# Hybrid decoder step on one core: x split ahead of the queries, q as three fp32r products, the norm broadcast ahead of u's 64-row tile, four gate jobs ahead of the state space products

## The reference

```
xn = rmsnorm(x, lp['norm1_g'])
u, q, k, v, qm, gates = jnp.split(xn @ lp['w_in'], split_at, axis=-1)
y_ssm, h_re, h_im = s5_scan(u, h0_re, h0_im, lp)
z = jax.nn.gelu(y_ssm)
z = z * jax.nn.sigmoid(z @ lp['w_glu'] + lp['b_glu'])
...
o_swa = sink_band_attention(q, kk, vv, True, lp['sinks'], rel_table)
o_mem = mem_attention(qm.reshape(...), mem_k, mem_v)
g = jax.nn.sigmoid(gates.reshape(b, t, N_BRANCHES, D_MODEL))
merged = (g[:, :, 0] * (z @ lp['w_br_ssm'])
          + g[:, :, 1] * (o_swa @ lp['w_br_swa'])
          + g[:, :, 2] * (o_mem @ lp['w_br_mem']))
x = x + merged @ lp['w_out']
x = x + hier_moe(rmsnorm(x, lp['norm2_g']), lp)
```

## Time and profile before

| | us |
|---|---|
| median of 3 runs (823.11 to 824.79) | 823.43 |
| profiled execution, its own time | 825.33 |
| its span, first to last instruction | 823.5 |
| TensorE busy | 764.2 (93%) |
| VectorE busy | 375.8 (46%) |
| ScalarE busy | 237.8 (29%) |
| GpSimd busy | 75.1 (9%) |

### The profile page before, as it was taken

One profiled execution on the slowest core, in us unless ns is written; L12 is line 12 of the kernel. 1 busy time (PEld: TensorE's weight loads), 2 busy tenths in 40 slices (PEclk: granted clock), 3 DMA queues, 4 the chain that ended last, 5 costly groups with the idle time before them and its releaser, 6 DMA issues. The chain is left out here.

```text
span 823.5 us, 11842 instructions
## 1 busy us (share of the span) xinstructions
PE 764.2 (93%) x4899; PEld 576.5 (70%) x4899; DVE 375.8 (46%) x677; ACT 237.8 (29%) x404; POOL 75.1 (9%) x105
## 2 busy tenths in 40 slices
PE   8999999999999999989999999998999978787864
PEld 6887899999998766779999988884333323222321
DVE  2589689903723666366244276454112111111117
ACT  1413531303563535262343232120111101100113
POOL 0100220001003020100000000011011110001000
PEclk9999999999999999999999999999999999999997
DMA  8652254314336452400241582089999999999957
GB/s 344 223 179 93 77 86 127 110 65 156 101 123 239 174 236 96 154 1 1 103 167 52 196 349 99 26 326 416 422 427 422 423 426 425 424 424 425 424 177 301
DMA packets 34554, 186.15 MB, mean 226 GB/s; under 512 B 5979, under 2 KB 6251, under 8 KB 17512
## 3 DMA queue, kind: packets, MB, share of 16 engines
q1 hardware_dynamic: 22288, 148.22, 44.9%
q0 software_dynamic: 11344, 35.24, 12.8%
q10 hardware_dynamic: 864, 1.88, 0.6%
HBM read 176.17 MB, written 17.22 MB: 235 GB/s over the span
## 5 line engine op out<-in xcount | busy, mean ns | idle before, releaser
L540 PE MATMUL ps<-sb 128*64 128x512 f32 (+16 forms) x2334 | 423.5, 436 | 47.9 <-DMA sb<-in_wexp 28.4
L540 PEld LDWEIGHTS ps<-sb 128*64 128x64 f32 (+6 forms) x2334 | 246.8, 160 | 198.9 <-issue 152.6
L540 PE MATMUL ps<-sr 128*128 128x288 f32 (+2 forms) x2160 | 302.6, 300 | 0.1
L540 PEld LDWEIGHTS ps<-sr 128*128 128x128 f32 x2160 | 289.8, 188 | 7.2 <-issue 1.4
L551 PEld LDWEIGHTS ps<-sb 128*128 128x128 f32 (+3 forms) x405 | 41.8, 140 | 31.9 <-issue 28.3
L2232 DVE SCALAR_TENSOR_TENSOR sb<-sb,ps 128x256 f32<-128x256 f32 x16 | 6.7, 421 | 124.9 <-ACT sb L1511 124.9
L551 PE MATMUL ps<-sb 128*128 128x128 f32 (+3 forms) x405 | 52.7, 269 | 3.1 <-issue 1.5
L1981 DVE TENSOR_TENSOR sr<-sb,sr 128x2048 fp32r<-128x2048 f32 (+2 forms) x23 | 39.9, 1754 | 28.4 <-ACT sr L1265 14.6
L2241 DVE COPY sb<-ps 128x1024 f32<-128x1024 f32 (+1 forms) x16 | 19.1, 1191 | 67.4 <-PE ps L540 67.4
L1969 DVE SCALAR_TENSOR_TENSOR sb<-sb,ps 128x576 f32<-128x576 f32 x24 | 18.1, 752 | 58.6 <-PE ps L540 58.6
L1173 ACT ACTIVATE sb<-ps 128x576 f32<-128x576 f32 (+4 forms) x29 | 22.9, 789 | 70.9 <-PE ps L540 48.9
(11 more groups left out here) (261 smaller groups left out, 465.1 us busy)
## 6 DMA issues: line engine op xcount, KB each, us to landing
sb<-in_wexp SPq DMA_DIRECT2D x96, 1024.0 KB, 27.5
sb<-in_wstream SPq DMA_DIRECT2D x33, 1024.0 KB, 4.9
sb<-in_mkT POOLq DMA_DIRECT2D x8, 512.0 KB, 9.9
sb<-in_mv POOLq DMA_DIRECT2D x8, 512.0 KB, 7.0
sb<-expert_rows SPq DMA_DIRECT2D x8, 512.0 KB, 7.5
sb<-in_x SPq DMA_DIRECT2D x4, 512.0 KB, 14.1
sb<-k_pad POOLq DMA_DIRECT2D x8, 256.0 KB, 6.1
sb<-in_x POOLq DMA_DIRECT2D x4, 512.0 KB, 9.6
```

The costliest lines, as they stand in the source:

```text
L540: return signed(nc.tensor.matmul(*a, **kw))
```

## The change

1. x is split in nine pieces instead of three, and earlier: the high parts on ScalarE behind u4's copy, the low parts on VectorE inside the input matrices, right behind the normed x.
2. Blocks 3 and 4 get high and low parts as well, and q0 to q3 become split jobs of 48 fp32r matmuls. q0 no longer waits slab by slab, but for all low parts of x and of block 3. kT stands between q0 and q1 as before.
3. rsb stands ahead of u4 on TensorE.
4. g00 and g01 stand ahead of K0, and g02 and g03 between K1 and VT0. g04 to g07 stay behind B3.
5. The low parts on VectorE: blocks 3 and 4 ahead of and between the tables of Y, 5 between those of VT, 6 and 7 behind the repacking of u, 8 behind B's copies, 9 behind the seventh `inside`, 10 behind the advances, 11 and 12 behind the scan. The high parts on ScalarE move alike; its wait for `scanned` stays behind g07.

```diff
-X_PARTS = [(O_XH, 0, 6 * T + TH), (O_SM, 6 * T + TH, TH), (O_SM + TH, 7 * T, T)]
-EARLY_HI = {5: O_Z + 256, 6: O_A + 8704, 7: O_A + 10752, 8: O_Z + 256, 9: O_A + 8704, 10: O_A + 10752, 11: O_O, 12: O_Z + 256}
+X_PARTS = [(O_XH + kt * T, kt * T, T) for kt in range(6)]
+X_PARTS += [(O_XH + 6 * T, 6 * T, TH), (O_SM, 6 * T + TH, TH), (O_SM + TH, 7 * T, T)]
+XS = [f"x{part}" for part in range(len(X_PARTS))]
+EARLY_HI = {3: O_UG, 4: O_A, 5: O_A + 2048, 6: O_UG, 7: O_A + 10752, 8: O_Z + 256, 9: O_A + 8704, 10: O_A + 10752, 11: O_O, 12: O_Z + 256}
...
-LOWS = [5, "x1", "x2", "x0"] + [what for what in HIGHS[4:] if not (isinstance(what, tuple) and what[0] == "w")] + [("w", b) for b in range(4)]
+LOWS = [what for what in HIGHS if not (isinstance(what, tuple) and what[0] == "w")] + [("w", b) for b in range(4)]
...
-    jobs = [f"u{t}" for t in range(TT)] + ["rsb"] + [f"kv{t}" for t in range(TT)]
-    jobs += ["q0", "kT"] + [f"q{m}" for m in range(1, 4)] + [f"K{i}" for i in range(2)]
+    jobs = [f"u{t}" for t in range(TT - 1)] + ["rsb", "u4"] + [f"kv{t}" for t in range(TT)]
+    jobs += ["q0", "kT"] + [f"q{m}" for m in range(1, 4)] + ["g00", "g01"] + [f"K{i}" for i in range(2)] + ["g02", "g03"]
-    jobs += [f"g0{d}" for d in range(8)] + [f"qm{m}" for m in range(4)] + [f"Y{i}" for i in range(4)]
+    jobs += [f"g0{d}" for d in range(4, 8)] + [f"qm{m}" for m in range(4)] + [f"Y{i}" for i in range(4)]
...
-            take("u4")
-            side_by_side("u4", O_XG, [(wu[0], 256), (wu[1], 256)]).then_inc(ps_ready, 1)
-            owed.append((w_used, 2))
...
+            take("u4")
+            side_by_side("u4", O_XG, [(wu[0], 256), (wu[1], 256)]).then_inc(ps_ready, 1)
+            owed.append((w_used, 2))
...
-            for m in range(4):
-                if m % 2 == 0:
-                    w = weights()
-                columns(f"q{m}", w + (m % 2) * 128, 256, O_X, KT).then_inc(ps_ready, 1)
-                if m == 0:
...
+            def turn_keys():
+                pe.wait_ge(kv_sb, TT)
+                take("kT")
+                for t in range(TT):
+                    last = turn_tile(pat(pair("kT"), t * 128, (1, ROWS[t])),
+                                     at(O_KV + t * 256, (1, 128), pn=ROWS[t]), at(O_ID, (1, ROWS[t]), pn=ROWS[t]))
+                last.then_inc(ps_ready, 1)
+
+            pe.wait_ge(lo_ready, LOWS.index(XS[-1]) + 1)
+            split_block(["q0", "q1"], turn_keys)
+            split_block(["q2", "q3"])
+            split_block(["g00", "g01"])
...
+            split_block(["g02", "g03"])
...
-            for d in range(0, 8, 2):
+            for d in range(4, 8, 2):
...
+            for part in range(7):
+                act.wait_ge(xn_ready, part + 1)
+                high_x(part)
...
+                if t == 0:
+                    act.wait_ge(lo_ready, 1)
+                    act.wait_ge(xn_ready, KT)
+                    high_x(7)
+                    high_x(8)
+                    early_high(3)
+                if t == 1:
+                    early_high(4)
...
-                    act.wait_ge(xn_ready, KT)
-                    high_x(0)
-                if m == 2:
-                    act.wait_ge(ssm_built, 2)
-                    high_x(1)
-                    high_x(2)
                     early_high(5)
+            early_high(6)
+            gate_zero(0)
+            gate_zero(1)
+            act.wait_ge(up_sb, 4)
+            early_high(7)
+            filled(act, "K1")
+            gate_zero(2)
+            gate_zero(3)
             for i in range(4):
                 copy_out(f"VT{i}", at(A_VT + i * 1024, (1, 1024)), pat(pair(f"VT{i}"), 0, (1, 1024)), vt_sb)
             for i in range(4):
                 copy_out(f"U{i}", at(O_UG + i * 8 * NC, (4 * NC, 2), (1, 4 * NC)),
                          pat(pair(f"U{i}"), 0, (512, 2), (1, 4 * NC)), ug_sb)
 
-            act.wait_ge(up_sb, 4)
-            early_high(6)
-            early_high(7)
-            for d in range(8):
-                filled(act, f"g0{d}")
-                c.free(fn(at(O_TH + d * T, (TH, 2), (1, TH)), pat(pair(f"g0{d}"), 0, (512, 2), (1, TH)), ACT.Tanh, scale=0.5),
-                       f"g0{d}")
+            early_high(8)
+            early_high(9)
+            for d in range(4, 8):
+                gate_zero(d)
+                if d == 5:
+                    early_high(10)
                 if d == 7:
                     act.wait_ge(scanned, 1)
-                if d % 2:
-                    early_high(8 + d // 2)
+                    early_high(11)
...
+            for part in range(len(X_PARTS)):
+                low_x(part)
...
+            early_low(3)
             for hf in range(2):
+                if hf:
+                    early_low(4)
...
             for hf in range(2):
+                if hf:
+                    early_low(5)
...
-            early_low(5)
-
-            filled(dve, "q3")
-            low_x(1)
-            low_x(2)
+            early_low(6)
...
-            low_x(0)
...
-            early_low(6)
+            early_low(8)
...
             for j in range(1, 8):
                 inside(j)
-                if j == 4:
-                    early_low(7)
-            early_low(8)
+            early_low(9)
             for k in range(1, 8):
                 advance((8 * k - 1) * G, (8 * k + 7) * G, c64)
-            early_low(9)
+            early_low(10)
...
-            for b in (10, 11, 12):
+            for b in (11, 12):
```

More of the change, by code:

```diff
@@ L558, in columns @@
                     for kt in range(kts):
-                        if job == "q0" and half == 0:
-                            pe.wait_ge(xn_ready, kt + 1)
                         last = mm(pat(p, half * 512, (1, TH)), at(w + kt * wstep, (1, 128)),
@@ L572, in split_columns, with split_block @@
                 return last
-            def split_block(jobs):
+            def split_block(jobs, between=None):
                 b = blocks_taken[0]
@@ L580, in split_block @@
                     split_columns(job, EARLY_HI[b] + i * 128, w + i * 128).then_inc(ps_ready, 1)
+                    if i == 0 and between:
+                        between()
                 owed.append((w_used, 1))
@@ L639, in _ @@
             pe.wait_ge(ld["const"], 16)
-            for m in range(4):
-                if m % 2 == 0:
-                    w = weights()
-                columns(f"q{m}", w + (m % 2) * 128, 256, O_X, KT).then_inc(ps_ready, 1)
-                if m == 0:
-                    pe.wait_ge(kv_sb, TT)
-                    take("kT")
-                    for t in range(TT):
-                        last = turn_tile(pat(pair("kT"), t * 128, (1, ROWS[t])),
-                                         at(O_KV + t * 256, (1, 128), pn=ROWS[t]), at(O_ID, (1, ROWS[t]), pn=ROWS[t]))
-                    last.then_inc(ps_ready, 1)
-                if m % 2:
-                    owed.append((w_used, 1))
+            def turn_keys():
[9 more added lines that the diff above has]
+            split_block(["g00", "g01"])
             pe.wait_ge(ssm_built, 1)
@@ L1201, in _, with gate_zero @@
                          scale=at(O_RS + t, (1, 1), pn=R))
+            def gate_zero(d):
+                filled(act, f"g0{d}")
+                c.free(fn(at(O_TH + d * T, (TH, 2), (1, TH)), pat(pair(f"g0{d}"), 0, (512, 2), (1, TH)), ACT.Tanh, scale=0.5),
+                       f"g0{d}")
             copy_sides("u4", A_US + 4 * 512, 256, u_sb)
+            for part in range(7):
+                act.wait_ge(xn_ready, part + 1)
+                high_x(part)
             for t in range(TT - 1):
@@ L1638, in _, with low_x, early_low @@
             dve.sem_inc(xn_ready, 1)
+            def low_x(part):
+                hi, src, n = X_PARTS[part]
+                dve.wait_ge(hi_ready, HIGHS.index(f"x{part}") + 1)
+                v.tensor_tensor(r32(O_X + src, n), at(O_X + src, (1, n)), r32(hi, n).bitcast(F32), ALU.subtract).then_inc(lo_ready, 1)
+            def early_low(b):
+                dve.wait_ge(hi_ready, HIGHS.index(b) + 1)
+                v.tensor_tensor(r32(raw_at(b), WB), at(raw_at(b), (1, WB)), r32(EARLY_HI[b], WB).bitcast(F32),
+                                ALU.subtract).then_inc(lo_ready, 1)
             dve.wait_ge(ld["ssm"], 16)
@@ L1709, in _ @@
                                    at(A_UC + i * 128, (CH, 8), (512, L), (1, CH), pn=NC)), up_sb)
-            early_low(5)
-            filled(dve, "q3")
-            low_x(1)
-            low_x(2)
+            early_low(6)
+            early_low(7)
             for i in range(2):
```

11 lines of the change are left out of this document (1 added, 10 removed).

## The result

| | us |
|---|---|
| changed kernel, median of 4 (831.55 to 835.52) | 833.5 |
| kernel before beside it, median of 4 (822.49 to 824.79) | 823.27 |
| ratio, 95% interval | 1.011, 1.0077 to 1.0142 |
| forecast, range | 826.8, 824.8 to 829.0 |

What follows compares the result with a forecast made beforehand. TensorE's queue of matmul jobs was taken to bound the front, each us counted in full. -5.6 (q) + 7.3 (wait before qm0) + 1.7 (clock) = +3.4 us on the 823.43 median gave 826.8 us, range 824.8 to 829.0.

Steps and rivals of the forecast that it cites:

- The q gain: On TensorE, four q jobs as three fp32r products take 6.37 instead of 7.76 us each: 5.6 us gained.
- q0, 0.7 us to spare: At q0, VectorE finishes block 3's low part at 58.0, TensorE arrives at 58.8: nothing lost.
- rival of an early fence: VectorE or ScalarE 1.5 us later at q0 or g00, added in full: 827.8 to 829.3 us; chance 0.14.
- its own signs of being wrong: In the changed kernel's profile, a TensorE hole under 4 us, or one at q0, would make the prediction wrong.
- g00 to g03: Gates ahead of the state space products: no wait; block 5's low part ready at 84.7, wanted at 85.2, 0.5 spare.
- steps 2 and 3: VectorE's low parts in time at q0 (0.7 us to spare) and at g00 (0.5 us): no wait at either.
- The hole before qm0: TensorE waits for block 9's low part: 32.7 us of VectorE chain after B against 25.5 of cover, 7.3 us.
- The clock: After the wait ahead of qm0, half clock for 3.4 us: 1.7 us lost, bounds nothing to 3.4.
- Y: hidden: Y0's wait for ScalarE's qm0 copy, ready at 182.1, hidden as TensorE comes at 184.3 or 186.0; otherwise 5.05 us.
- The sum: Whole kernel: -5.6 + 7.3 + 1.7 = +3.4 us, Y starting near 186, median 826.8 us.
- steps 2 and 5: The q0 fence, put at nothing lost, and the clock after qm0's wait, put at 1.7 us.
- What the front gains or loses moves it as a whole: Expert stage, weight-paced but released by the front, shifts with it; every us of the front counted at full price.

Runs made afterwards that it cites:

- before_again: Kernel before the change, unaltered, run again for a second trace: 824.57 us, ratio 0.9991 to the kernel before.
- e4: Changed kernel with 54 fp32r matmuls nobody reads put in TensorE's hole ahead of qm0: 827.07 us, ratio 1.0025 to the kernel before.
- e8: Changed kernel with six unread fp32 matmuls ahead of TensorE's wait for the second expert pair's gathered rows: 831.73 us, ratio 1.0089 to the kernel before.
- e7: Changed kernel with block 3's low part moved ahead of VectorE's four last input-matrix instructions: 830.04 us, ratio 1.0066 to the kernel before.
- e5: Changed kernel with low parts of blocks 3, 8, 9, 10 (high parts 8, 9) earlier, qm copies before the scan wait: 822.05 us, ratio 0.9964.
- e10: Kernel of e5 with the six filling matmuls of e8 in the expert stage: 822.01 us, ratio 0.9968 to the kernel before.
- e9: Same kernel as e5, run again: 821.93 us, ratio 0.9970 to the kernel before.
- e1: Changed kernel with block 9's low part moved from behind the scan's seventh inner step to behind the fourth: 826.9 us, ratio 1.0005 to the kernel before.
- after_again: Changed kernel, unaltered, run again for a second profile: 831.56 us, ratio 1.0073 to the kernel before.
- e3: Kernel before the change with 32 unread fp32r matmuls put ahead of Y: 827.39 us, ratio 1.0028 to the kernel before.
- e6: Changed kernel's q split alone, with g00 to g03 back behind B and low and high parts placed for that order: 829.24 us, ratio 1.0077.

## Why the prediction was wrong, point by point

**1. The q gain: right.** 6.35 us a job, for 7.76 in the earlier trace rows. The Trainium skill's four passes for true FP32 ("FP8 and Floating Point Precision", TensorE Precision Notes) would have put three of them at 5.82, an estimate; the trace again has 0.82 and not 0.75 of the fp32 job.

**2. q0, 0.7 us to spare: the step that failed.** VectorE's chain was right in length: 18.0 us from the start of the norm products to block 3's low part, 18.0 measured. Its start, 39.98, and TensorE's arrival, "TensorE reaches q0 at 58.8 as before", were single readings from one trace. Norm products began at 39.9 to 40.8 in the seven profiles; the last k/v copy is at 57.55 in before_again and at 57.35 in the changed kernel. Two engines that don't slide together were subtracted, in an execution in which TensorE was late and VectorE early. Measured: a hole of 1.65, 2.77, 1.39 (e4) and 0.75 us (e8), with 1.5 us of clock behind the 2.77. The prediction's rival of an early fence had the place and, with 1.5 us, nearly the price, at a chance of 0.14; the table above makes it the likely case. A hole at q0 was also one of its own signs of being wrong.

**3. g00 to g03: no hole, but by luck.** With q0 late, g00 had its part in time by some 0.1 us, not 0.5. Where block 3's part is moved ahead and q0 starts at 57.1 to 57.5, g00 waits 0.6 to 1.6 us (e7, e5, e10, e9). Only with a late TensorE, as in e1, are both fences met. Taken as one, steps 2 and 3 miss that VectorE's chain paces TensorE as far as g00.

**4. The hole before qm0: right.** 7.20, 7.14, 7.19 and 7.17 us against 7.3, block 9's low part last, whatever the front did; e1 took it away by moving that part alone. From the end of B to the end of block 9's low part it was 32.7 us, as summed.

**5. The clock: right in kind, too small.** 1.7 forecast. 4.3 us of work at 0.50 is 2.2 lost, e4 has 2.1 to 2.5. This term of the sum was mis-sized by some 0.5 us. The size was taken from another place, where less standing came ahead; it lies between the bounds given. The Trainium skill ("TensorE: Matmul & The Clock Gate", Part 1) has the half rate as what an idle TensorE falls to, and the trace agrees, with 0.50.

**6. Y: hidden, as said.** Once qm0's hole is closed it shows, 0.72 us in e1, small since block 10's hole stood in for it, a fence that the step skipped.

**The sum.** At Y, from the same start: -5.6 + 1.65 + 7.2 + 2.2 = +5.4, measured 5.4; in the second profile with an earlier start -5.6 + 2.77 + 1.5 + 7.14 + 2.3 - 1.0 = +7.1, measured 7.2. The forecast had +3.4, so steps 2 and 5 are short by 2 to 4 us at Y.

**What the sum left out: the expert stage, put at nothing.** "What the front gains or loses moves it as a whole" was taken as all that happens there. In the first profiled execution the stand for the second pair's rows and its half clock add 5.9 us, more than any step's error. Part of this is scatter: the changed kernel's second profile has a stand of 1.48 us at full clock. But not all of it need be. From the first expert product to the end of the span it is 259.7 to 260.9 us in the four profiles with g00 to g03 behind B (before, before_again, e3, e6), and 261.0 to 266.3 in all ten with them ahead of K and VT. For the average I have only an estimate: the changed kernel's fourteen executions have a mean of 831.9 and the three profiles with its front a mean Y of 187.3 (first, after_again, e8), so 644.6 us lie behind Y; for the kernel before it is 824.7 over 84 executions less 182.0 over two profiles, 642.7. Of some 7 us between the two kernels, about 5 would then be the front and 2 the expert stage. What in the change does it is open: landings of 9.3 us and more came only with the split q jobs (in eight profiles of eleven, in none of three without), but no experiment separates them from chance, and e3, with one profile and ten executions, shows no such loss from a shift by itself. The first four executions lie some 2 us above the later ten, and nothing here explains that.

## What to carry over

When a margin between two engines is under 2 us, take the time of each from more than one execution, or ask what happens if only one of them moves: a fence with 0.7 us to spare by one profile was a hole in six of seven. Preparatory work put ahead of a dependent chain has to be followed to each consumer behind it, not only to the first that becomes late: closing qm0's hole showed block 10's, closing q0's showed g00's and gained nothing. "The rest moves as a whole" is a term too, and wants a second trace like any other. And where a split's parts make a wait, move the parts before giving up the split: the same jobs went from 1.0073 to 0.997.
